# Per-head sums of a recurrence: one float32 product each, or two products in the rounded format

## The reference

```python
kk = heads(k * k_k).astype(jnp.float32)
kk = kk / jnp.maximum(jnp.sqrt(jnp.sum(jnp.square(kk), axis=-1, keepdims=True)), 1e-12)
...
k = k * (1.0 + (a - 1.0) * k_a)
...
y = delta_rule_scan(r_h, heads(decay), k_h, v_h, -kk, kk * a_h)
mean = jnp.mean(y, axis=-1, keepdims=True)
var = jnp.mean(jnp.square(y - mean), axis=-1, keepdims=True)
y = ((y - mean) * lax.rsqrt(var + GN_EPS)).reshape(B, T, MIX_WIDTH)
...
bonus = (jnp.sum(r_h * k_h * r_k, axis=-1, keepdims=True) * v_h).reshape(B, T, MIX_WIDTH)
return (y + bonus) * g, q_mem
```

## Time and profile before

| what | us |
|---|---|
| median of 3 runs | 1216.94 (1216.67 to 1217.26) |
| the profiled execution's own time | 1216.83 |
| its span, first to last instruction | 1214.7 |
| TensorE busy with products | 1113.4 (92% of the span) |
| VectorE busy | 650.8 (54%) |
| ScalarE busy | 456.3 (38%) |
| GpSimd busy | 11.9 (1%) |

### The profile page before, as it was taken

How to read it: one execution, slowest core, us unless ns; L and a number is a source line. 1 busy time by engine, 2 the same in 40 slices (tenths; PEclk the granted TensorE clock), 3 DMA queues, 4 the chain that set the end, 5 groups by cost and what they waited for, 6 DMA issues and landing times.

```text
span 1214.7 us, 21885 instructions
## 1 busy us (share of the span) xinstructions
PE 1113.4 (92%) x9476; PEld 828.7 (68%) x9476; DVE 650.8 (54%) x1057; ACT 456.3 (38%) x736; POOL 11.9 (1%) x12
## 2 busy tenths in 40 slices
PE   6999999677699897999998989899899999999998
PEld 4277776254457566776776766667688888888887
DVE  2378777885625657475856655564533323333322
ACT  3233344245642355243241413342554312454211
POOL 0000000000000000000000000000000000000000
PEclk9999999789999898999999999999899999999999
DMA  8831222300003221011011004022232332332330
GB/s 327 302 122 54 102 70 90 119 1 1 1 20 120 70 70 53 20 37 36 21 37 38 20 2 175 2 62 95 55 102 87 104 103 88 89 102 87 104 113 26
DMA packets 25581, 94.93 MB, mean 78 GB/s; under 512 B 2832, under 2 KB 2832, under 8 KB 24976
## 3 DMA queue, kind: packets, MB, share of 16 engines
q1 hardware_dynamic: 25488, 93.54, 23.8%
HBM read 89.34 MB, written 4.19 MB: 77 GB/s over the span
## 4 chain that ended last, share of the span: by engine, by line
PE 54%; DVE 5%; ACT 2%; issue 1%; ACTq 0%; DVEq 0%
PE psum L689 14%; PE psum L690 13%; PE psum L691 13%; PE psum L699 4%; PE psum L987 2%; PE psum L1000 1%; PE psum L1036 1%; PE psum L955 1%; PE psum L1003 1%; PE psum L1079 1%; DVE work L2064 1%; PE psum L977 1%; PE psum L1059 1%; PE psum L1070 1%; PE psum L1013 1%
## 5 line engine op out<-in xcount | busy, mean ns | idle before, releaser
L1669 DVE TENSOR_TENSOR weights_low<-ring,weights_high 128x1024 fp32r<-128x1024 f32 x72 | 88.2, 1225 | 82.9 <-ACT weights_high L1334 82.9
L1334 ACT ACTIVATE weights_high<-ring 128x1024 fp32r<-128x1024 f32 x72 | 75.9, 1055 | 127.7 <-PE psum L691 127.7
L689 PE MATMUL psum<-normed_high,weights_high 128*128 128x512 f32 x256 | 102.6, 401 | 5.1 <-DVE normed_low L1674 4.5
L690 PE MATMUL psum<-normed_low,weights_high 128*128 128x512 f32 x256 | 101.9, 398 | 0.0
L691 PE MATMUL psum<-normed_high,weights_low 128*128 128x512 f32 x256 | 101.8, 398 | 0.0
L690 PE MATMUL psum<-hidden_low,weights_high 128*128 128x512 f32 x256 | 99.6, 389 | 0.0
L689 PE MATMUL psum<-hidden_high,weights_high 128*128 128x512 f32 x256 | 99.6, 389 | 0.0
L691 PE MATMUL psum<-hidden_high,weights_low 128*128 128x512 f32 x256 | 99.6, 389 | 0.0
L1284 ACT ACTIVATE work<-psum 128x384 f32<-128x384 f32 (+2 forms) x124 | 58.3, 511 | 88.8 <-PE psum L1036 48.8
L689 PE MATMUL psum<-pair_normed_high,pair_weights_high 128*128 128x512 f32 x176 | 77.1, 438 | 12.3 <-DVE normed_low L1674 4.3
L2149 DVE TENSOR_TENSOR hidden_low<-work,hidden_high 128x512 fp32r<-128x512 f32 x32 | 22.2, 693 | 110.2 <-ACT hidden_high L1579 110.2
(11 more groups left out here) (235 smaller groups left out, 2100.2 us busy)
## 6 DMA issues: line engine op xcount, KB each, us to landing
ring<-weights SPq DMA_DIRECT2D x154, 512.0 KB, 3.6
residual<-xT SPq DMA_DIRECT2D x1, 2048.0 KB, 18.5
residual_saved<-residual SPq DMA_DIRECT2D x8, 256.0 KB, 2.0
residual<-residual_saved SPq DMA_DIRECT2D x1, 2048.0 KB, 8.9
outT<-residual SPq DMA_DIRECT2D x8, 256.0 KB, 3.2
work<-memT SPq DMA_DIRECT2D x1, 1024.0 KB, 5.0
work<-ctxT SPq DMA_DIRECT2D x1, 1024.0 KB, 9.8
small_sb<-small SPq DMA_DIRECT2D x1, 907.0 KB, 7.7
```

Source lines behind the costliest of these rows:

```text
L689: pe.matmul(out, wh, high(k), start=first and n == 0, stop=False)
L690: pe.matmul(out, wh, low(k), start=False, stop=False)
L1334: act.activation(WH[group(q)][:, q % 2, :], ring[:, SLOT[b], :], ACT.Copy).then_inc(w_high, 1)
L1669: vec.tensor_tensor(WL[group(q)][:, q % 2, :], ring[:, SLOT[b], :], WH[group(q)][:, q % 2, :].bitcast(F32), ALU.subtract).then_inc(w_low, 1)
```

## The change

The sums `kks`, `bon` and `gv` (six of each, 18 in all) are made by `split_sum`: instead of one float32 product, an fp32r product with a rounded copy of the tile and an fp32r product with the rest, added in PSUM. The table `heads` is rounded once, ahead of pair 0. For every sum ScalarE gets one copy of 128x512 into fp32r, and VectorE one subtraction of 128x512 that waits for that copy. The square goes to HS as before, and ScalarE waits for its end before it copies.

```diff
@@ -421,6 +421,11 @@
         NT, Y, MAK, MRK = map(heads_first, (NT, Y, MAK, MRK))
         TK, TV = map(pairs_first, (TK, TV))
 
+        SPLIT_SUMS_AT = half + 17 * S
+        SUM_H = [over(f"sum_high{i}", "work", SPLIT_SUMS_AT + 2 * i * S, P, S) for i in range(3)]
+        SUM_L = [over(f"sum_low{i}", "work", SPLIT_SUMS_AT + (2 * i + 1) * S, P, S) for i in range(3)]
+        HEADS_R = over("heads_rounded", "work", SPLIT_SUMS_AT + 6 * S, P, P)
+
         inputs = 10 * S
         QM = region(inputs, 2, S)
         MPT = region(inputs + 2 * S, 2, SM)
@@ -510,6 +515,9 @@
         partial = sem("shift_partial")
         low_used = sem("tanh_placed")
         scan_done, exps_done = sem("log_decays_ready"), sem("decays_ready")
+        heads_rounded = sem("heads_rounded")
+        kk_high, bonus_high, gn_high = sem("kk_high_ready"), sem("bonus_high_ready"), sem("gn_high_ready")
+        bonus_low = sem("bonus_low_ready")
         kk_sq, kk_rs, bonus_in = sem("kk_squares"), sem("kk_rstd"), sem("bonus_in")
         ab_ready = sem("a_and_b_ready")
         gt_ready = sem("transitions_ready")
@@ -928,13 +936,20 @@
                 for h, x in enumerate("wA"):
                     one(f"{x}_{p}", SV[rows(h), LORA_AT + p * P:LORA_AT + (p + 1) * P], TZ[rows(h), :])
 
+            def split_sum(name, i):
+
+                out = take(name)
+                pe.wait_ge(heads_rounded, 1)
+                pe.matmul(out, HEADS_R[:], SUM_H[i][:], start=True, stop=False)
+                full_inc(pe.matmul(out, HEADS_R[:], SUM_L[i][:], start=False, stop=True), name)
+
             def kk_sum(p):
                 pe.wait_ge(kk_sq, p + 1)
-                one(f"kks_{p}", tab("heads"), HS[:, 0, :])
+                split_sum(f"kks_{p}", 0)
 
             def bonus_sum(p):
-                pe.wait_ge(bonus_in, p + 1)
-                one(f"bon_{p}", tab("heads"), T2)
+                pe.wait_ge(bonus_low, p + 1)
+                split_sum(f"bon_{p}", 1)
 
             def gn_mean(p):
                 pe.wait_ge(*is_free(f"yh_{p}"))
@@ -942,7 +957,7 @@
 
             def gn_square(p):
                 pe.wait_ge(gn_sq, p + 1)
-                one(f"gv_{p}", tab("heads"), HS[:, 1, :])
+                split_sum(f"gv_{p}", 2)
 
             def gate_low_rank(p):
                 pe.wait_ge(sig_out, sig_at["gd_sig"][0] + 1)
@@ -1475,7 +1490,8 @@
                 if p:
 
                     act.wait_ge(*is_full(f"kks_{p - 1}"))
-                act.activation(HS[:, 0, :], K0, ACT.Square, scale=col("k_k", p)).then_inc(kk_sq, 1)
+                link(act.activation(HS[:, 0, :], K0, ACT.Square, scale=col("k_k", p)))
+                act.activation(SUM_H[0][:], HS[:, 0, :], ACT.Copy).then_inc(kk_high, 1)
                 shift_start(f"r_{p}", MU_PAIR + 3 * p + 1, R0)
 
             def key_norm(p):
@@ -1492,17 +1508,30 @@
                     act.wait_ge(*is_free(f"bon_{p - 1}"))
                 shift_start(f"v_{p}", MU_PAIR + 3 * p + 2, V0)
 
+            def bonus_rounded(p):
+
+                act.wait_ge(bonus_in, p + 1)
+                if p:
+                    act.wait_ge(*is_full(f"bon_{p - 1}"))
+                act.activation(SUM_H[1][:], T2, ACT.Copy).then_inc(bonus_high, 1)
+
             def gn_squares(p):
                 act.wait_ge(*is_free(f"gm_{p}"))
-                act.activation(HS[:, 1, :], CAT[:, p, :], ACT.Square).then_inc(gn_sq, 1)
+                if p:
+                    act.wait_ge(*is_full(f"gv_{p - 1}"))
+                link(act.activation(HS[:, 1, :], CAT[:, p, :], ACT.Square))
+                act.activation(SUM_H[2][:], HS[:, 1, :], ACT.Copy).then_inc(gn_high, 1)
 
             def gn_rstd(p):
                 rms(f"gv_{p}", HR[:, 1, :], S, 1.0 / DH, GN_EPS, gn_rs)
 
+            act.activation(HEADS_R[:], tab("heads"), ACT.Copy).then_inc(heads_rounded, 1)
             pair_inputs(0)
+            bonus_rounded(0)
             key_norm(0)
             pair_values(0)
             pair_inputs(1)
+            bonus_rounded(1)
             key_norm(1)
             for p in range(NP):
                 if p:
@@ -1524,6 +1553,8 @@
                         memory_unit(2 * LEVELS.index(b) + 1)
                     if p + 1 < NP and b == LEVELS[1]:
                         pair_values(p + 1)
+                        if p:
+                            bonus_rounded(p + 1)
                 for h in range(HEADS):
                     copy_out(f"wu_{p}_{h}", WU[:, :, h, :], src=bank(f"wu_{p}_{h}").rearrange("p (c n) -> p c n", c=G))
                 if p + 2 < NP:
@@ -1928,6 +1959,18 @@
                 vec.wait_ge(*is_free(f"r_{p}"))
                 scaled_product(T2, R0, col("r_k", p), QW[:]).then_inc(bonus_in, 1)
 
+            def kk_low(p):
+                vec.wait_ge(kk_high, p + 1)
+                vec.tensor_tensor(SUM_L[0][:], HS[:, 0, :], SUM_H[0][:].bitcast(F32), ALU.subtract).then_inc(kk_sq, 1)
+
+            def bonus_rest(p):
+                vec.wait_ge(bonus_high, p + 1)
+                vec.tensor_tensor(SUM_L[1][:], T2, SUM_H[1][:].bitcast(F32), ALU.subtract).then_inc(bonus_low, 1)
+
+            def gn_low(p):
+                vec.wait_ge(gn_high, p + 1)
+                vec.tensor_tensor(SUM_L[2][:], HS[:, 1, :], SUM_H[2][:].bitcast(F32), ALU.subtract).then_inc(gn_sq, 1)
+
             def least_norm(p):
                 vec.wait_ge(*is_full(f"kks_{p}"))
                 free_inc(vec.tensor_scalar(HR[:, 0, :], bank(f"kks_{p}"), KK_LEAST, None, ALU.max), f"kks_{p}")
@@ -1998,6 +2041,8 @@
                     pair_input(p, x)
                     weights_after(p, x)
                 changed_key(p)
+                bonus_rest(p)
+                kk_low(p)
                 least_norm(p)
                 if p == 0:
                     pair_input(0, "v")
@@ -2031,6 +2076,7 @@
 
                     if p and b == LEVELS[0]:
                         gn_centre(p - 1)
+                        gn_low(p - 1)
                     if b == LEVELS[0 if p == NP - 1 else 1]:
                         vec.wait_ge(*is_full(f"ka_{p}"))
                         vec.tensor_tensor(MAK, by_head(f"ka_{p}")[:, :, :, 0], mask("before", HEADS, G), ALU.mult)
@@ -2044,6 +2090,7 @@
                             changed_key(late)
                             decayed_r(late)
                             weights_after(late, "r")
+                            bonus_rest(late)
                     if p + 1 < NP and b == LEVELS[2]:
                         pair_input(p + 1, "v")
                     if p + 1 < NP and b == LEVELS[3]:
@@ -2109,6 +2156,7 @@
                         if n == 5:
                             weights_after(p + 2, "k")
                 if p + 2 < NP:
+                    kk_low(p + 2)
                     pair_input(p + 2, "r")
                 vec.wait_ge(*is_free(f"yu_{p}"))
                 vec.wait_ge(*is_full(f"yh_{p}"))
@@ -2119,6 +2167,7 @@
                     memory_queries(1)
             memory_unit(MU_CHAIN + len(CHAIN))
             gn_centre(NP - 1)
+            gn_low(NP - 1)
             for n in range(3):
                 mixed_low(n)
             weights_low(SPLIT_AT["mix0"])
```

## The result

| | before | changed |
|---|---|---|
| median of 6 runs, us | 1216.81 (1215.26 to 1219.07) | 1255.64 (1249.51 to 1257.13) |
| profiled execution, us | 1216.83 | 1255.83 |
| its span, us | 1214.7 | 1253.7 |
| mean granted clock | 0.978 | 0.962 |

The changed kernel is slower: 1.0298 times the kernel before (95% interval 1.0277 to 1.0318), 38.8 us at the medians and 36.3 (33.7 to 38.7) by the ratio. Forecast were 1247 and a range of 1235 to 1257.

The account below looks back on a forecast made before the run. The prediction took TensorE to bound the loop (busy 56.76 of 60 us per turn), but not the preparation of pairs 0 and 1. 1216.8 + 27.0 for waits and savings + 3.0 for the clock gave 1247 us, range 1235 to 1257.

Parts of the forecast that it names:

- Level 2, +1.95 each: Turns of pairs 1 to 5: VectorE's additions start 1.95 us later, waiting in gn_low for square and copy; +9.75 in all.
- Level 4, +2.9 each: Turns of pairs 1 to 4: T2's copy queues behind v's drain, delaying the y products of level 8; +11.6 us in all.
- Preparation, +7.9: Preparing pairs 0 and 1: later kks sums delay the chain through ScalarE and VectorE by 7.9 us (7.0 to 8.6).
- lower end of 1234: Whole kernel: 1234 us without any fall of the clock and with every lower bound.
- Savings, -3.0 and -1.0: Cheaper sums on TensorE: gv of pairs 0 to 4 saves 3.0 us, kks of pairs 2 to 5 saves 1.0.
- bon gives nothing: Level 16: cheaper bon sums save 0 (bounds 0 and -0.6 us each), as VectorE's additions start right behind its own work.
- Tail, +1.7: Pair 5: gn_low ahead of VectorE's full list moves everything by 1.95 less 0.23 us, +1.7.
- The clock, +3.0: TensorE's granted clock falls after two of the new waits, 1.5 us each: +3.0 us (0 to 10).
- Waits and savings: All terms but the clock's: -3.0 - 1.0 + 9.75 + 11.6 + 7.9 + 1.7 = +27.0 us.
- The likeliest case of the prediction: New waits at TensorE with one to four falls of its clock: 1247 us, chance 0.50.
- its last sign of being wrong: After each new wait, TensorE's clock stays low much longer than one 4 us window at 0.57 (3.4 us at half speed).
- a fall at most of the nine waits: Rival for the loop's level 2 and 4 waits: seven clock falls at 1.5 us make 10.5, 1254 us; chance 0.13.

Follow-up runs that it names:

- The kernel with gn_low moved: The changed kernel with gn_low, VectorE's subtraction for gv, placed behind the additions of level 2 instead of ahead of them: 1238.8 us, ratio 1.0159 to the kernel before.
- The passes alone: The kernel before with two fp32r products per sum, no copies or subtractions, and the sums' low part left out: 1212.6 us, ratio 0.9954.
- The fillers: The changed kernel with products nobody needs put into TensorE's list where it waits, in pairs 0 to 4 and pair 5: 1245.0 us, ratio 1.0228.

## Why the prediction was right, and where it was off

- **Level 2, +1.95 each.** Right: the additions start at 543.17, 1.96 after the centring's end at 541.21 (0.04 before the change), and TensorE is 2.17 late where it was 0.25. The kernel with gn_low moved shows it is this wait.
- **Level 4, +2.9 each.** Right: 2.85. The kernel with the copy ahead of v's drain shows that its place in ScalarE's list is the cause.
- **Preparation, +7.9.** The mechanism is right, the size short. The turn of pair 0 starts 7.3 later, but TensorE came into this stretch 1.5 us earlier (it waited up to 446.83 for the product that the earlier trace rows has at 448.34), so that 8.8 are lost in it, 0.2 above the upper bound. One piece had been left to the bounds: the subtraction of T2's rest took 1.20 and not 0.69, in pair 0 as in pair 1, as it ended only after GpSimd's product. Another was in no term: the wait for kks of pair 0 brought the clock down, so that VectorE took its result up only 1.24 us after the sum began (the two rows below). By the lock that the Trainium skill describes (SBUF — State Buffer, "SBUF: two separate sides") the subtraction waits until GpSimd's product has ended. The trace agrees within 0.2 us: the product ends at 481.34, and the subtraction at 481.89, where 0.69 behind the product would be 482.03. The recorded sum has two slips, both small: its steps for pair 0 add up to 456.7 and not 457.0, and its lower end of 1234 counts bon five times where there are six, which is 0.6 too high.

TensorE and VectorE of the changed kernel, kks of pair 0, and VectorE's norm behind the last pair:

```profile
455.71 0.78 PE L943 MATMUL psum<-sum_high,heads_rounded 128*128 128x512 f32 x1 [3.19 <-DVE sum_low L1964]
```

```profile
456.95 0.69 DVE L1976 TENSOR_SCALAR head_rstd<-psum 128x512 f32<-128x512 f32 x1 [1.30 <-PE psum L944]
...
840.12 0.75 DVE L1626 SCALAR_TENSOR_TENSOR mixed<-mixed,small_sb,head_rstd 128x512 f32<-128x512 f32 x1
```

- **Savings, -3.0 and -1.0.** The passes alone gave 5.6 (3.0 to 8.2), so -4.0 has the right size. That bon gives nothing wasn't measured by itself; the 0.7 of the turn of pair 1 leave no room for its 0.6 beside gv's. kks gave 0.2 in the turn of pair 0. Inside the changed kernel they are worth more, 11 us, which I had not foreseen.
- **Tail, +1.7.** Seen in its place: VectorE takes the norm behind the last pair at 840.12 without idle time before it, where the earlier trace rows had 0.23. In this turn the clock hides the amount. The kernel with gn_low moved and the one with gv undone show it at 1.00: 59.87 against 58.71, which is 1.2 net, or 1.8 with the 0.6 that gv of pair 4 saves. TensorE waits 2.03 us for gv of pair 5 (0.65 before), and in the changed kernel the clock falls behind that too (0.71 from 836 us to the output projection).
- **The clock, +3.0.** This is the term that was mis-sized. I had taken two falls at 1.5. The price was about right (2.7 for the two in the turn of pair 1), the count was not: the clock fell behind eight of the nine waits, behind those for kks of pair 0 and gv of pair 5, and for 10.4 us at level 16 of pair 5. The windows give 7.0 us at 1.2 GHz in the turns of pairs 1 and 2 each, 3.5 in that of pair 3, 7.4 in that of pair 4 and 16.6 in that of pair 5, against none, none, none, 3.4 and none before. I had set the waits of 1.95 aside as too short, and pair 5, whose products have gaps anyway, wasn't looked at.
- **What the clock cost.** Waits and savings made 27.0, which leaves 9 (by the ratio) to 12 us (at the medians) of the change's cost. The fillers gave back 8.5 to 10.7. That they end so near the sum, 1245.0 against 1243.8, is in part luck: turn by turn that kernel lies 3.9, 4.7, 2.1, 2.3 and 9.1 us above the kernel before, where the sum has 4.0 four times and 3.1. Against pair 5 with its fillers and its clock stand the gap that the kernel before had in pair 3 and its own fall in pair 4. An estimate from the windows is higher: the turns have 38 us more at 1.2 GHz than before, and at the price of pair 1, 2.7 for 7.0 us, that is about 15. So the clock cost three to five times the 3.0, near or above the 10 of its upper bound.
- **The range.** The likeliest case of the prediction, one to four falls, did not occur, and its last sign of being wrong, a clock that stays low for much longer than one such window, did occur in pair 5. The rival "a fall at most of the nine waits", 1254, was right in the count and came closest, and had 0.13. That my own range still holds the result, near its upper end, is luck in that part: the upper bounds of all the other terms were added too, and those did not all come out at their upper ends.

## What to carry to other kernels

When an operation gets a helper on another engine, look at what is queued behind the instruction that waits for the helper: here 1.4 us of copy and subtraction cost 2 to 3 us per use, since additions that TensorE was waiting for stood behind them, and moving one line gave 17 us back. Count the room at the reader (0.25 us for kks, 0.3 at level 4) before counting the saving at the product. And where TensorE is the bound, a new wait of 2 us or more should be charged again for the clock, at each place where it stands: here a fall came behind eight of nine, at about 1.35 us each. A stretch that has gaps already can then stay slow for long, and did so in some of these kernels and not in others.

## What the runs showed of the hardware

- Products that nobody needs, put into waits, made the kernel 10.7 us faster at the medians (1245.0 against 1255.6) and 8.5 by the ratios, though one wait of 2.4 us stayed unfilled.
- TensorE's granted clock fell after waits of 2.17 and 2.85 us in the same turn (0.57 in the 4 us behind each, 0.94 over 58.5 us), where before the change waits of 0.25 us left it at 1.00.
- In the turn of pair 5, where waits of 1.4 and 1.3 us stand 5 us apart, one kernel had 59.9 us at 1.00 and another, whose turn differs by one move, 69.0 at 0.88, of which 10.4 us at 1.2 GHz right behind those waits.
- A wait of 2.41 us in that turn was followed by 3.4 us at 1.2 GHz in one kernel and by 17 in another, with the same list there.
- A VectorE subtraction of 128x512 took 1.20 us beside GpSimd's product of 1.27, and 0.69 without.
